# Attention units at experts 23, 32, 40, 45, 53 and 58, with two lists' exponentials beside them, and block 4's list three experts sooner

## Chip, cores and metric

The kernel runs on one core of a Trainium2 chip. The metric is device microseconds of that core; lower is better. Three runs of the kernel before took 1696.72 to 1699.43 us, with a median of 1698.52.

## What is computed

One step of a one-layer decoder, all in float32. There are 512 prompt tokens (four tiles of 128) and 8 sequences of 8 sample tokens (one tile of 64). A token mixer (sliding-window attention with 8 heads beside a gated MLP) and a cross-attention over 256 memory tokens are followed by a retrieval of experts, which takes most of the time:

```python
def block(xt):                                       # 128 tokens
    q = (xt @ w_pq).reshape(128, 8, 2, 128)
    s = einsum('thcd,hckd->thck', q, sub_keys)       # scores of 2 x 128 keys per head
    s1, i1 = top_k(s[:, :, 0], 16); s2, i2 = top_k(s[:, :, 1], 16)
    top, sel = top_k(s1[..., :, None] + s2[..., None, :], 16)
    gate = softmax(top)                              # idx: the 16 chosen of 128*128 experts
    h = einsum('td,thkd->thk', xt, u_tab[idx])
    return einsum('thk,thkd->td', gelu(h) * gate, v_tab[idx])
```

Each token and head has its own 16 rows of the two expert tables. The attention of the prompt tiles 2 to 4, which the change moves, is a softmax over a band of 256 keys with a learned sink per head, and then an RMS norm of its rows.

## The kernel before

**Lists and experts.** The retrieval is cut into 36 lists (the program's `BLOCKS`) of 16 experts. Lists 0 to 3 serve the sample tile, two heads at a time on the two halves of the partitions; then eight lists, one per head, serve each prompt tile. An expert of the program, numbered g = 16 b + k from 0 to 575, is one column of a list: 128 tokens, each with one row of 2048 floats (u and v side by side), so 1 MiB. Every engine runs the same loop over g, and each does its share:

- GpSimd issues the indirect gather (line 684) into one of the slots, after it has waited for the list's indices (`idx_ready`, once for each list) and for the product that used the slot before (`v_used`). `slot_table` (line 407) hands out the slots; from expert 31 to 73 there are eight in turn, so gather g follows the product of expert g - 8.
- VectorE waits for the landing and takes the dot with the token rows (line 1543).
- ScalarE takes Gelu (line 954), multiplies with the gate (958) and writes a 64-wide diagonal (963): `diagonal`, line 949.
- TensorE adds diagonal times v rows to the tile's sum, eight matmuls at line 2118. Its end is `v_used`.

**What is written between them.** The rest of the work stands in the same loops at expert numbers written out by hand. A list n is selected while earlier ones run: `query_at(n)` (line 452) is (n - 2)*16 plus `LATE`, and `query_steps` gives the steps counted from there. TensorE computes the queries at steps 0 to 7 (line 1878), transposes at 9 and scores at 11; ScalarE copies at 9, 11 and 13; VectorE sorts the two key halves at 15 and 16 (`top_keys`, lines 1330 to 1334), takes the best pairs at 18 (`best_pairs`, line 1342, from 1348 to 1351), the experts' indices at 20 (`experts_of`, line 1353; its last instruction, 1371, is `idx_ready`) and finishes the gates at 23 (`finish_gates`, line 1374). ScalarE takes the exponentials of the gates at step 21 (`gates`, line 859), at the head of the expert, ahead of its diagonal. With `LATE` 8 for list 4 its steps start at expert 40: indices at 60, exponentials at 61, finished at 63.

**The six attention units** (`UNIT_AT`, line 430) are tiles 2, 3 and 4, with four heads each. Counted from a unit's expert: TensorE's scores at 0; VectorE's mask and maximum at 4 (four of line 1478, three small ones); ScalarE's exponentials at 5 (line 934), after the diagonal; TensorE's transposes at 6 (line 2080), ScalarE's copies at 8 (940, 941), TensorE's products with the values at 9 (2087), VectorE's scaled output at 12 (1497). A tile's second unit also has the norm of its rows on ScalarE at 13 (lines 945, 946), VectorE's scaling at 16 (`attn_scaled`, line 1319), TensorE's transposes at 18 (1909) and VectorE's `attn_take` at 21 (line 1325). The second unit of the next tile waits for it (`n_T`) ahead of its transposes at 6:

```python
                    if r == 1:
                        pe.wait_ge(n_T, t - 1)
```

**Other work there.** Tile 1's norm ahead of its experts (`ffn`): ScalarE at expert 28 (lines 768, 769), after any unit's work of that expert; VectorE at 30 (lines 1300 and 1305), which waits for it; TensorE's transposes at 31 and 34 (2010) and ScalarE's copies at 33 and 36 (907). On VectorE the steps of a list come before those of a unit of the same expert. ScalarE's functions Gelu, Exp and Sqrt each need their table; a load (ACT_TABLE_LOAD) stands ahead of the first call after another of the three. SP's queue reloads x rows and `w_piece` after unit 5's norm.

Of the kernel before, what the change touches and what calls it, by code (L numbers as in the profile page):

```python
# [117 lines left out]
def hybrid_step(nc, I, O):  # L118
    ctx = ExitStack()
    with ctx:  # L120
# [23 lines left out]
        def bank(n, w=512):  # L144
            return ps[:, n * 512:n * 512 + w]

        def v3(ap, a):
            return ap.rearrange("p (a b) -> p a b", a=a)
# [278 lines left out]
        QUERY_AT = {1: 6, 2: 134, 3: 208, 4: 218}  # L427
        CROSS_AT = {1: 9, 2: 138, 3: 222, 4: 244}
        FFN_AT = {1: 28, 2: 158, 3: 268, 4: 16 * 23 + 2}
        UNIT_AT = (24, 31, 38, 44, 51, 57)  # L430
        OUT_AT = (77, 81, 85, 91, 95, 99, 105, 109, 113, 119, 123, 127)

        LATE = {2: 9, 4: 8, 12: 7}
        QUICK = (2, 12)

        def half_bank(t):
# [15 lines left out]
        def query_at(s):  # L452

            return (s - 2) * TOPK + LATE.get(s, 0)

        def query_steps(g):

            steps = []
            for s in range(BLOCKS):
                d = g - query_at(s)  # L460
                if s in QUICK and 0 <= d < KD // 2:
                    steps += [(s, 2 * d), (s, 2 * d + 1)]
                elif s in QUICK and KD // 2 <= d < 2 * TOPK:
                    steps.append((s, d + KD // 2))
                elif s not in QUICK and 0 <= d < 2 * TOPK:
                    steps.append((s, d))
            return steps

        def units():

            return ((2 + u // 2, u % 2, u, at) for u, at in enumerate(UNIT_AT))

# [217 lines left out]
        def _(act):  # L690
# [27 lines left out]
            def gates_out(t):  # L718

                act.wait_ge(pgu_done, NTH[t])  # L720
                if t == ORDER[0]:
                    act.wait_ge(mkv_done, 2)
                act.wait_ge(x_rstd, NTH[t])
                r = gate_rows(t)
                act.activation(gu_rows(t)[r], bank(gates_bank(t))[r], ACT.Gelu, scale=rs_x[r, t:t + 1]).then_inc(gu_out, 1)
# [31 lines left out]
            def half_norm(t):  # L757

                act.wait_ge(sgu_out, TILES if t == 3 else t + 1)
                spare = gv_rows(4 if t == 3 else t)  # L760
                chain(act.activation(spare, gu_rows(t), ACT.Square, accum_out=ss_g[:, t:t + 1]))
                act.activation(ss_g[:, t:t + 1], ss_g[:, t:t + 1], ACT.Sqrt, bias=eps[:, 0:1], scale=1.0 / 512)\
                   .then_inc(h_std, 1)
# [81 lines left out]
            def queries_out(s):  # L845
                act.wait_ge(pq_q, s + 1)
                act.activation(q_sb, bank(4)[:, 0:256], ACT.Copy).then_inc(pq_qo, 1)

            def queriesT_out(s):
                act.wait_ge(pq_t, s + 1)  # L850
                act.activation(qT_sb, v3(bank(5)[:, 0:256], 2), ACT.Copy).then_inc(pq_to, 1)

            def scores_out(s):
                act.wait_ge(pq_s, s + 1)
                if s > 0:
                    act.wait_ge(best_ready, s)
                act.activation(ss, v3(bank(5)[:, 256:512], 2), ACT.Copy).then_inc(pq_so, 1)  # L857

            def gates(s, m):

                act.wait_ge(best_ready, s + 1)
                act.activation(gate[:, m, :], bestv, ACT.Exp, bias=negtop, accum_out=esum).then_inc(gexp_ready, 1)  # L862
# [34 lines left out]
            def ffn(t, part):  # L897

                if part == 0:
                    act.wait_ge(l_add, 2 * t)  # L900
                    if t >= 2:
                        act.wait_ge(u_used, tile_end(t - 2))
                    row_norm(t, xn(t), f_std, ss_f)
                elif part in (5, 8):
                    h = (part - 5) // 3
                    act.wait_ge(f_tr, 2 * t + h)
                    act.activation(expert_T(t)[:, 4 * h:4 * h + 4, :], v3(bank(6), 4), ACT.Copy).then_inc(f_out, 1)
# [21 lines left out]
            def unit(t, r, u, step):  # L929

                if step == 5:
                    act.wait_ge(a_max, u + 1)
                    for i in range(4):
                        act.activation(U_s[:, i, :], U_s[:, i, :], ACT.Exp, bias=nmx[:, 4 + i:5 + i],
                                       accum_out=rs[:, 4 + i:5 + i])
                    act.activation(es[:, 4:8], es[:, 4:8], ACT.Exp).then_inc(a_exp, 1)
                elif step == 8:
                    act.wait_ge(a_pT, u + 1)
                    act.wait_ge(*((a_pv, u) if u > 0 else (l_pv, 2)))
                    act.activation(U_p[:, 0:4, :], v3(bank(7), 4), ACT.Copy).then_inc(a_pTo, 1)  # L940
                    act.activation(U_p[:, 4:8, :], v3(bank(6), 4), ACT.Copy)\
                       .then_inc(a_pTo, 1)
                elif step == 13 and r == 1:
                    act.wait_ge(a_o, 2 * (t - 1))
                    chain(act.activation(U_p[:, 0:4, :], v3(OU, 4), ACT.Square, accum_out=ss_a[:, t:t + 1]))
                    act.activation(ss_a[:, t:t + 1], ss_a[:, t:t + 1], ACT.Sqrt, bias=eps[:, 0:1], scale=1.0 / 512)\
                       .then_inc(n_std, 1)

            def diagonal(b, k):

                g = b * TOPK + k
                col = slice(k, k + 1)
                act.wait_ge(u_used, g + 1)
                act.activation(hgelu[:, b % 2, col], hdot[:, b % 2, col], ACT.Gelu).then_inc(gelu_ready, 1)  # L954
                if k == 0:
                    act.wait_ge(gate_ready, b + 1)
                act.wait_ge(gelu_ready, g + 1)
                act.activation(coef[:, b % 2, col], gate[:, b % 4, col], ACT.Copy, scale=hgelu[:, b % 2, col])\  # L958
                   .then_inc(coef_ready, 1)
                if g >= DIAGS:  # L960
                    act.wait_ge(v_used, g - DIAGS + 1)
                act.wait_ge(coef_ready, g + 1)
                act.activation(diag[:, g % DIAGS, :], fold[:, 0:HALF], ACT.Copy, scale=coef[:, b % 2, col])\  # L963
                   .then_inc(diag_ready, 1)

            def final(t):

                act.wait_ge(acc_added, t + 1)
                spare = expert_T(1 if t == 3 else 2)
                chain(act.activation(spare, v3(xr(t), KD), ACT.Square, accum_out=stat[:, 64 + t:65 + t]))  # L970
                act.activation(stat[:, 64 + t:65 + t], stat[:, 64 + t:65 + t], ACT.Sqrt, bias=eps[:, 0:1],
                               scale=1.0 / D).then_inc(fin_std, 1)

            act.wait_ge(ld_ffn, 32)
            for b in range(BLOCKS):
                for k in range(TOPK):
                    g = b * TOPK + k
                    for n, step in query_steps(g):
                        if step == 9 and n > 1:
                            queries_out(n)  # L980
                        if step == 11 and n > 1:
                            queriesT_out(n)
                        if step == 13 and n > 1:
                            scores_out(n)
                        if step == 21:
                            gates(n, n % 4)
                    if k == 9 and b in FINAL_SLOT:
                        final(FINAL_SLOT[b])
                    diagonal(b, k)
                    if g == 2:  # L990
                        gates_out(3)
                    if g == 6:
                        gates_out(4)
                    if g == 8:
                        half_norm(3)
                        half_norm(4)
                    if g == 9:
                        qkT_evac(3)
                    if g == 11:
                        qkT_evac(4)  # L1000
                    for t, at in CROSS_AT.items():
                        cross(t, g - at)
                    for t, r, u, at in units():
                        unit(t, r, u, g - at)
                    for t in PREP_AT:
                        if g == PREP_AT[t]:
                            prep(t, 0)
                        if g == QUERY_AT[t] + 2 + (t > 1):
                            prep(t, 3)
                    for t, at in FFN_AT.items():  # L1010
                        ffn(t, g - at)
# [1173 lines left out]
```

## Time and profile before

| | |
|---|---|
| median of three runs | 1698.52 us |
| the profiled execution | 1697.96 us |
| its span, first to last instruction | 1696.2 us |
| granted TensorE clock, mean | 0.861 |
| bytes moved by GpSimd's queue | 604.28 MB, 86.3% of 16 DMA engines' time |
| HBM read | 653.24 MB; 388 GB/s over the span with the writes |
| experts (GpSimd's gathers at line 684) | 566 into R, 10 into x_res |

The experts' loop begins at 172.8 us, with the first gather. The profile gives busy time of the engines, a table of any stretches, and a timeline of each engine in which an instruction's idle time before it and what ended that stand in brackets. A dot (line 1543) is written in the text with its expert's number, which is its place in the order of those instructions.

### The profile page before, as it was taken

The numbers are of one execution on the slowest core, as the hardware profiler recorded it, in microseconds if no ns is written. First come the engines' busy times: TensorE is split into PE (matmuls) and PEld (weight loads), VectorE is DVE, ScalarE is ACT, GpSimd is POOL, SyncE is SP. The second block draws the span as 40 slices with busy tenths as digits, with TensorE's granted clock in tenths as the row PEclk, the third lists the DMA queues.
The fourth block names the chain that finished last, engine by engine and source line by source line (L and its number), as shares of the span: only waits on it lengthen the run. The fifth ranks groups of instructions, "written<-read, shape, count | busy, mean of one in ns | idle before, by whom it ended". The sixth has DMA issues, their size and how long they took to land.

```text
span 1696.2 us, 21662 instructions
## 1 busy us (share of the span) xinstructions
PE 1307.6 (77%) x7069; PEld 474.2 (28%) x7069; DVE 1165.1 (69%) x2798; ACT 806.8 (48%) x2337; POOL 656.4 (39%) x584
## 2 busy tenths in 40 slices
PE   9998987877888777678787776777677677766776
PEld 4454442333344222123232111212112111111110
DVE  2545749797667676777777677677666676777764
ACT  1424456774445454455555454445444445444443
POOL 0000234434534344444444444444444444444441
PEclk9999998989999788988988777877878877788865
DMA  9426799999999999999999999999999999999995
GB/s 359 165 100 251 274 388 420 414 374 421 420 421 421 417 394 414 422 405 412 421 420 421 421 421 421 421 422 420 421 421 422 421 406 421 422 421 420 421 418 220
DMA packets 97441, 657.88 MB, mean 388 GB/s; under 512 B 12512, under 2 KB 15584, under 8 KB 20768
## 3 DMA queue, kind: packets, MB, share of 16 engines
q0 software_dynamic: 83056, 604.28, 86.3%
q1 hardware_dynamic: 14272, 52.21, 8.0%
q8 instruction: 56, 0.92, 0.2%
q14 instruction: 57, 0.47, 0.1%
HBM read 653.24 MB, written 4.19 MB: 388 GB/s over the span
## 4 chain that ended last, share of the span: by engine, by line
DMA 44%; PE 25%; DVE 12%; ACT 11%; issue 7%; POOL 1%; ACTq 0%; DVEq 0%; POOLq 0%
DMA R<-in_peer_uv,R 42%; PE ps L2118 9%; PE ps L1624 5%; DVE R L1543 5%; PE ps L1878 3%; ACT L954 2%; ACT R L963 2%; ACT R L958 1%; PE ps L1595 1%; DVE R L1331 1%; ACT R L954 1%; DVE R L1332 1%; DVE R L1334 1%; ACT L862 1%; POOL R L684 1%
## 5 line engine op out<-in xcount | busy, mean ns | idle before, releaser
L2118 PE MATMUL ps<-R 64*64 64x512 f32 x4528 | 741.5, 736 | 355.8 <-ACT R L963 355.6
L684 POOL DMA_INDIRECT R<-in_peer_uv,R x566 | 643.6, 1137 | 830.7 <-PE ps L2118 754.1
L1543 DVE CUSTOM_DVE_ANT_0 R<-R 128x1024 f32<-128x1024 f32 x566 | 687.8, 1224 | 374.1 <-DMA R<-in_peer_uv,R 370.3
L954 ACT ACTIVATE R<-R 128x1 f32<-128x1 f32 x576 | 115.8, 201 | 602.0 <-DVE R L1543 600.7
L2118 PEld LDWEIGHTS ps<-R 64*64 64x64 f32 x4528 | 136.4, 151 | 710.2 <-ACT R L963 624.2
L963 ACT ACTIVATE R<-R 128x64 f32<-128x64 f32 x576 | 200.4, 348 | 54.9 <-ACT R L958 1.9
L1878 PE MATMUL ps<-A,R 128*128 128x256 f32 (+1 forms) x640 | 221.0, 470 | 0.7 <-ACT R L839 0.7
L958 ACT ACTIVATE R<-R 128x1 f32<-128x1 f32 x576 | 169.7, 295 | 20.9
L1878 PEld LDWEIGHTS ps<-A,R 128*128 128x128 f32 (+1 forms) x640 | 94.8, 198 | 256.1 <-issue 253.1
L1624 PE MATMUL ps<-A,R 128*128 128x512 f32 (+1 forms) x256 | 100.7, 545 | 0.4 <-ACT R L735 0.4
L1595 PE MATMUL ps<-R 128*128 128x256 f32 (+2 forms) x352 | 79.8, 382 | 0.0
L954 ACT ACT_TABLE_LOAD x61 | 78.3, 1283 | 1.5 <-DVE R L1543 0.5
L1595 PEld LDWEIGHTS ps<-R 128*128 128x128 f32 x352 | 60.9, 202 | 23.5 <-issue 15.5
L1624 PEld LDWEIGHTS ps<-A,R 128*128 128x128 f32 x256 | 47.2, 190 | 47.0 <-issue 43.5
L684 POOL DMA_INDIRECT x_res<-in_peer_uv,R x10 | 10.4, 1036 | 119.2 <-DVE R L1383 109.3
L1543 DVE DVE_READ_ACCUMULATOR2_ANT R<- 128x1 f32 x576 | 47.4, 82 | 0.0
L862 ACT ACT_TABLE_LOAD x34 | 43.6, 1283 | 0.6
L1333 DVE MAX8 R<-R 128x8 f32<-128x128 f32 (+1 forms) x106 | 36.1, 340 | 3.7
L1330 DVE MAX8 R<-R 128x8 f32<-128x128 f32 (+1 forms) x106 | 35.7, 337 | 1.5 <-ACT R L857 0.3
L1331 DVE FIND_INDEX8 R<-R 128x8 uint32<-128x128 f32 (+1 forms) x106 | 35.0, 330 | 0.0
L1334 DVE FIND_INDEX8 R<-R 128x8 uint32<-128x128 f32 (+1 forms) x106 | 35.0, 330 | 0.0
L1332 DVE MATCH_REPLACE8 R<-R 128x128 f32<-128x128 f32 (+1 forms) x106 | 34.0, 321 | 0.0
(304 smaller groups left out, 947.5 us busy)
## 6 DMA issues: line engine op xcount, KB each, us to landing
R<-in_peer_uv,R POOLq DMA_INDIRECT x566, 15.6
A<-in_w_pq SPq DMA_DIRECT2D x8, 1024.0 KB, 9.8
A<-in_w_in SPq DMA_DIRECT2D x3, 2048.0 KB, 20.2
R<-in_w_out SPq DMA_DIRECT2D x4, 1024.0 KB, 9.0
x_res<-in_x_prompt SPq DMA_DIRECT2D x6, 512.0 KB, 8.6
R<-in_w_out_rows SPq DMA_DIRECT2D x1, 3072.0 KB, 9.9
R<-in_x_promptT SPq DMA_DIRECT2D x4, 512.0 KB, 7.3
R<-in_w_cq SPq DMA_DIRECT2D x2, 1024.0 KB, 10.7
```

What stands on the lines that cost most here:

```text
L684: pool.indirect_dma_start(slots[slot_of[g]], None, I["peer_uv"][:, :], bass.IndirectOffsetOnAxis(ap=idx[:, b % 4, k:k + 1], axis=0)).then_ ...
L862: act.activation(gate[:, m, :], bestv, ACT.Exp, bias=negtop, accum_out=esum).then_inc(gexp_ready, 1)
L954: act.activation(hgelu[:, b % 2, col], hdot[:, b % 2, col], ACT.Gelu).then_inc(gelu_ready, 1)
L958: act.activation(coef[:, b % 2, col], gate[:, b % 4, col], ACT.Copy, scale=hgelu[:, b % 2, col])\
L963: act.activation(diag[:, g % DIAGS, :], fold[:, 0:HALF], ACT.Copy, scale=coef[:, b % 2, col])\
L1331: chain(dve.max_index(inds[:, 0:8], vals[:, 0:8], values))
L1334: return dve.max_index(inds[:, 8:16], vals[:, 8:16], values)
L1543: dve.tensor_tensor_reduce(u, u, xn(t), 1.0, 0.0, ALU.mult, ALU.add, hdot[:, b % 2, k:k + 1]).then_inc(u_used, 1)
L1595: ins = pe.matmul(out, lhs(k), rhs(k), start=(k == 0), stop=(k == n - 1))
L1624: ins = pe.matmul(out_bank[:, 0:CHUNKS[c][1] - CHUNKS[c][0]], tile_T(t)[:, k, :], w_in[c][:, k, :], start=(k == 0), stop=(k == KD - 1))
L1878: ins = pe.matmul(bank(4)[rows, 0:256], expert_T(t)[:, k, :], w_pq(h)[:, k, :], start=(k == 0), stop=(k == KD - 1))
L2118: ins = pe.matmul(bank(2 * (t % 2) + q)[rows], diag[tokens, g % DIAGS, :], v_rows[slot_of[g]][tokens, c * 512:(c + 1) * 512], start=first, ...
```

## The change

The units start at experts 23, 32, 40, 45, 53 and 58 instead of 24, 31, 38, 44, 51 and 57. List 4's steps start at 37 instead of 40. Exponentials of a list's gates that are due at the expert at which a unit's exponentials stand are taken just ahead of those, behind the diagonal and not ahead of it; with these numbers that holds for list 3 (expert 37, unit 1) and list 4 (expert 58, unit 4).

```diff
-        UNIT_AT = (24, 31, 38, 44, 51, 57)
+        UNIT_AT = (23, 32, 40, 45, 53, 58)
         OUT_AT = (77, 81, 85, 91, 95, 99, 105, 109, 113, 119, 123, 127)
 
-        LATE = {2: 9, 4: 8, 12: 7}
+        LATE = {2: 9, 4: 5, 12: 7}
...
+            def exps_beside(g):
+
+                return any(g - at == 5 for at in UNIT_AT)
+
...
-                        if step == 21:
+                        if step == 21 and not exps_beside(g):
                             gates(n, n % 4)
...
                     for t, r, u, at in units():
+                        for n, step in query_steps(g):
+                            if step == 21 and g - at == 5:
+                                gates(n, n % 4)
                         unit(t, r, u, g - at)
```

## Rows read from the trace of the kernel before

**Rows 1.** The page, busy time of the engines and share of the span.

```profile
PE 1307.6 (77%) x7069; PEld 474.2 (28%) x7069; DVE 1165.1 (69%) x2798; ACT 806.8 (48%) x2337; POOL 656.4 (39%) x584
```

**Rows 2.** Table by stretches: length, busy us (count) by engine, PEclk, DMA share, GB/s.

```profile
360.00:365.00 5.00, 3.87 (x19) 1.16 (x20) 4.83 (x15) 4.60 (x14) 1.96 (x2) 0.66 0.30 102
365.00:370.00 5.00, 4.77 (x44) 2.84 (x42) 4.76 (x19) 4.69 (x12) 3.75 (x5) 1.00 0.96 357
370.00:375.00 5.00, 1.04 (x9) 0.16 (x8) 4.76 (x16) 4.83 (x15) 2.37 (x2) 1.00 1.00 400
...
434.00:574.00 140.00, 118.66 (x668) 57.20 (x664) 93.90 (x221) 58.61 (x181) 56.53 (x50) 0.93 1.01 421
```

**Rows 3.** Line 684, issue to landing; GpSimd's timeline: start, us, instruction [idle <-releaser].

```profile
DMA to landing us min/median/max: 5.5/15.1/20.8
...
312.05 0.94 POOL L684 DMA_INDIRECT R<-in_peer_uv,R  x1 [1.72 <-PE ps L2118]
...
362.73 1.14 POOL L684 DMA_INDIRECT R<-in_peer_uv,R  x1 [9.01 <-DVE R L1371]
...
380.13 0.94 POOL L684 DMA_INDIRECT R<-in_peer_uv,R  x1 [7.09 <-PE ps L2118]
```

**Rows 4.** TensorE's timeline, 300 to 400 us.

```profile
315.49 0.70 PE L1878 MATMUL ps<-A,R 128*128 128x256 f32 x2
...
375.97 1.94 PE L2080 MATMUL ps<-ident,R 128*128 128x128 f32 x8 [4.93 <-DVE R L1325]
```

**Rows 5.** VectorE's timeline, 270 to 384 us.

```profile
273.06 1.22 DVE L1543 CUSTOM_DVE_ANT_0 R<-R 128x1024 f32<-128x1024 f32 x1
...
281.96 0.16 DVE L1300 RECIPROCAL stat<-stat 128x1 f32<-128x1 f32 x1
...
283.35 1.22 DVE L1543 CUSTOM_DVE_ANT_0 R<-R 128x1024 f32<-128x1024 f32 x1
...
296.27 0.42 DVE L1478 CUSTOM_DVE_ANT_0 R<-ps,band 128x256 f32<-128x256 f32 x1
...
302.51 1.21 DVE L1543 CUSTOM_DVE_ANT_0 R<-R 128x1024 f32<-128x1024 f32 x1
...
314.57 0.49 DVE L1497 TENSOR_TENSOR R<-ps,stat 128x128 f32<-128x128 f32 x2 [0.20 <-PE ps L2087]
...
320.54 1.23 DVE L1543 CUSTOM_DVE_ANT_0 R<-R 128x1024 f32<-128x1024 f32 x1 [1.25 <-DMA R<-in_peer_uv,R]
...
342.89 1.23 DVE L1543 CUSTOM_DVE_ANT_0 R<-R 128x1024 f32<-128x1024 f32 x1 [1.24 <-DMA R<-in_peer_uv,R]
...
352.83 1.22 DVE L1543 CUSTOM_DVE_ANT_0 x_res<-x_res,R 128x1024 f32<-128x1024 f32 x1
...
357.06 1.23 DVE L1543 CUSTOM_DVE_ANT_0 R<-R 128x1024 f32<-128x1024 f32 x1
...
359.77 0.17 DVE L1355 TENSOR_SCALAR R<-R 128x16 uint32<-128x16 uint32 x1
...
362.38 0.16 DVE L1319 RECIPROCAL stat<-stat 128x1 f32<-128x1 f32 x1
...
375.14 0.69 DVE L1325 TENSOR_TENSOR R<-ps,gains 128x512 f32<-128x512 f32 x1
```

**Rows 6.** ScalarE's timeline, 264 to 420 us.

```profile
280.27 0.29 ACT L769 ACTIVATE stat<-stat,eps 128x1 f32<-128x1 f32 x1
...
300.54 1.28 ACT L934 ACT_TABLE_LOAD   x1
301.83 0.51 ACT L934 ACTIVATE R<-R,stat 128x256 f32<-128x256 f32 x1
...
306.08 0.20 ACT L954 ACTIVATE R<-R 128x1 f32<-128x1 f32 x1
...
355.60 0.20 ACT L954 ACTIVATE R<-R 128x1 f32<-128x1 f32 x1
...
360.10 0.20 ACT L954 ACTIVATE R<-R 128x1 f32<-128x1 f32 x1
```

## Prediction

> **What bounds the kernel now.** I read the page's busy shares first. No compute engine is above 77% [rows 1], so a wait or a transfer sets the end. The table by stretches says which: from expert 82 on (434 to 574 us) the gathers move 421 GB/s with all 16 DMA engines busy [rows 2]. At 1 MiB each that is 2.49 us per expert, and the vector engine's dots show the same pace. Bytes are fixed, so from expert 20 on the end moves only by the time the DMA engines stand empty. Near the attention units they do so once: 102 GB/s in 360 to 365, 357 and 400 in the next two stretches [rows 2]. (421-102)x5 + (421-357)x5 + (421-400)x5 kB over 421 GB/s is 4.8 us. So the change can win about 4.8 us, 0.28%, while a loss has no such cap. A measurement of this kernel tells about 0.2%, 3.4 us, from no change.
>
> GpSimd's timeline says who made the hole: after gather 63 it waits 9.01 us for L1371, list 4's indices, and issues gather 64 at 362.73 [rows 3]. The same view holds a second cause behind the first. With eight slots in turn, gather g reuses the slot of expert g-8 and waits for its product. Gather 71 goes out at 380.13 after 7.09 us of waiting for TensorE. TensorE was late there because unit 5's transposes waited 4.93 us for L1325 [rows 4], unit 3's `attn_take`, which VectorE reached at 375.14, busy in nearly all of each stretch from 360 on [rows 2, 5].
>
> **The loop as a budget.** VectorE waited on landings for experts 46 and 55 (320.54, 342.89) [rows 5]; that fixes the undisturbed landing of any expert g: 342.89 + 2.49(g-55). Gather 71 is due on VectorE at 382.7; issued at 380.13 after a loss of 4.8 it came at 387.5, a lead of 7.3 us. Bounds: the shortest issue to landing is 5.5 [rows 3]; gather 46 had 8.5 (312.05 to 320.54) and nothing was lost. I take 7.3, from a row in which the stream was just cut. A gather issued later than its due time less 7.3 costs the excess.
>
> **Removed: table loads.** One load is 1.28 us and the next instruction starts 0.01 us behind it (300.54, 301.83 [rows 6]). Gelu, Exp and Sqrt each reload. Unit 0's exponentials (now at expert 28) stand before tile 1's norm: one load fewer. Unit 1's norm and unit 2's exponentials meet at 45: one fewer. Unit 3's norm, list 4's and unit 4's exponentials meet at 58: three instead of six. List 3's exponentials already followed unit 1's with no load between (experts 36 and 37), so that half of the edit buys nothing. In all 5x1.28 = 6.4 us of ScalarE. I keep 6.4, from the rows. The Trainium skill (ScalarE: Activation LUTs, "What ACT_TABLE_LOAD costs") puts 2.66 us on a switch, a drain included, which would make it 13.3 us; the rows show no drain. ScalarE is off the path most of the time; what counts is where its blocks now stand.
>
> **Moved: the first region, experts 28 to 46.** Today the norm's square root is out at 280.56 and VectorE, arriving at 281.96, does not wait [rows 5, 6]. After: unit 0's scores at expert 27 put dot 28 at 276.3 (273.06 + 1.15 + 2.0; the unit step is four L1478, 0.35 apart, and three small ones of 0.2 [rows 5]). ScalarE then does diagonal 28 (to 278.5), load and exponentials (3.6), square (1.2), load and root (1.6): root out at 284.8. VectorE stands from 281.3, and dot 31 starts at 286.4 instead of 283.35: 3.0 late. From there to dot 37 it has no gap (283.35 to 302.51, 19.2 us [rows 5]) and the same steps to do, so dot 37 starts at 305.5. The unit's exponentials, which today run at 300.54 while VectorE is busy [rows 6], now stand behind diagonal 37: 307.8, plus the 5.1 us that the block takes today (300.54 to 306.08 less a 0.5 us copy), so Gelu 38 is at 312.9 and diagonal 38 at 313.8. Product 38 ended at 311.8, just ahead of gather 46 [rows 3]; it will end at 315.0, or 315.9 if TensorE's granted clock has fallen (it stood idle; the stretch 360 to 365 shows 0.66 after such a pause, at the 1.2 GHz level for part of it [rows 2]). Gather 46 is issued 0.3 later, due 320.54 - 7.3 = 313.2. Loss 2.1 to 3.0; I take 2.6. Unit 1's output scaling then waits for TensorE where it waited 0.20 us (314.57 [rows 5]): about 5 us of VectorE pause at expert 44. The landings, late too, and seven light experts absorb it by 52.
>
> **Moved: the second region, experts 52 to 72** (times as if the first cost nothing). List 4's index is ready after dot 57. From dot 52 at 335.4 VectorE has six dots (6.9), two key sorts (3.7), best pairs (dot 58 at 352.83, 1.15 long, to dot 59 at 357.06: 3.1), experts_of (359.77 to 362.38, 2.6 [rows 5]) and unit steps (3.9): index at 353.1, dot 58 at 355.6. Due for gather 64 is 365.3 - 7.3 = 358.0, so the 9.01 us wait is gone and with it this hole. But all of list 4's selection, unit 3's outputs and unit 4's scores now precede dot 58, which was at 352.83. Behind it ScalarE has one block: the diagonal (1.0), the norm (355.60 to 360.10 today, less that and a load: 2.2), and gates and exponentials as a 5.1 us block like the one above: 8.3 us from Gelu 58 to Gelu 59 [rows 6]. The gates' sums are out 4.9 us after Gelu 58 (356.9: 1.0 + 2.2 + 1.3 + 0.4), at 361.8; `finish_gates` at dot 60 wants them at 359.1. VectorE waits 2.7 us for gates that today are taken before diagonal 61, with no norm and no unit ahead of them. Dot 61 at 362.1; five dots (5.8), two sorts for list 5 (3.7), unit steps (3.5): dot 66 at 375.1. `attn_take` has moved from 65 to 66, and there stands behind best pairs of list 5: 1.15 + 3.1 + 0.6, done at 380.0 instead of 375.8. Unit 5's transposes, the held product and the next gather follow as they do today, 375.97 to 380.13, 4.2 us [rows 3, 4]: gather 72 is issued at 384.2, due 385.2 - 7.3 = 377.9. Loss 6.3; waits of VectorE for TensorE on the way, the kind that shows as 0.20 us today and grows to 5 in the first region, may add 1.5. I take 7.0.
>
> **Queues.** SP's reload of `w_piece` waits for unit 5's norm, now at expert 71, and feeds a product at 77: its bytes are the same, six experts cover it, and without them it costs TensorE one expert, 2.5 us. List 4's query products on TensorE (37 to 44 instead of 40 to 47) and its three copies on ScalarE keep their number; they lie in waits for diagonals. Without that cover the products cost 0.70 us an expert (315.49 [rows 4]). GpSimd only gains list 4's index earlier.
>
> **Sum.** 2.6 + 7.0 - 4.8 = +4.8 us. The profiled execution took 1697.96 (span 1696.2), 0.6 below the median of the runs; on the median's scale 1703.2.
>
> **Rivals.**
> 1. The stall only changes its name. The first region's delay is absorbed by gathers already queued (lead nearer 5.5), and gather 72 takes over from 64: 7.0 - 4.8 = +2.2, or zero if the pauses are smaller, 1698 to 1701. For it: today's gather 71 was nearly as late as 64, two causes of one hole. Against: gather 46 has only 1.1 us to spare.
> 2. Faster. List 4's work falls into pauses of VectorE (1.24 us before dot 55 [rows 5], more before 54), the saved loads bring products 59 to 64 forward, and no new wait comes: the hole closes by up to 4.8 us, 1693.7. It decides at one point: gather 72 issued by 378. Against it: a grouped block waits for the latest of its inputs and holds up every diagonal behind it. The Trainium skill's rule to group calls by table set (ScalarE: Activation LUTs, "Table sets: the hidden batching unit") is this rival: by it, fewer switches win.
> 3. Both pauses are worse (slow clock at product 38 and 59, exponentials of unit 4 delaying unit 5's scores): 4 + 8.5 - 4.8 = +7.7, 1706.
>
> **Chances.** My forecast with rival 3, 0.57 (0.45 and 0.12); rival 1, 0.30; rival 2, 0.13. Beyond 0.2%: slower 0.57, faster 0.13, within 0.30. The range runs from rival 1's lower end (1698) to rival 3's (1706), each with 2 to 2.5 us for the bounds of the lead and the clock: 1695.5 to 1708. Within my own case: 1701.5 to 1705.
>
> **What would show it.** Right: five fewer table loads on ScalarE; the 9.01 us wait on L1371 gone; L1300 at expert 30 behind a pause of 3 to 4 us for ScalarE; gather 46 at 315 to 316 and a dip of GB/s near 315 to 320; VectorE waiting for L862 at `finish_gates` of list 4; L2080 waiting for L1325 before product 64 and a dip after 370. Wrong: 420 GB/s through both stretches, or dot 37 still at 302.5. Then the end would be 4 to 5 us earlier, not later.

## The result and the profile after

The change made the kernel slower: 1708.65 us, median of five runs (1704.59 to 1715.74), against 1698.52 (1696.72 to 1701.47, five runs beside them). The ratio is 1.0066, with a 95% interval of 1.0044 to 1.0089. Run a second time, beside the experiments, it was 1710.0 against 1700.48: 1.0051, 1.0037 to 1.0065. So the change costs 9.5 to 10.1 us by the medians (8.7 to 11.2 by the ratios) where I forecast 4.8. The sign was right, the size was half, and 1708.65 lies 0.65 above my range.

The profiled execution of the changed kernel took 1715.74 (span 1714.0), the highest of its five times and 7.1 above their median. Its own difference to the one of before, 17.8 us, is therefore larger than the change's cost. The change's second profiled execution took 1717.29, again the longest of its group, and shows the same waits as the first within 0.2 us. So the traces of the change show it at its slow end, while the profiled executions of the other kernels below lie within 3.3 us of their medians. I use the traces for where and why, and the medians for how much. Lines of VectorE and TensorE stand seven lower in the code than before (L1543 is L1550, L2118 is L2125); ScalarE's up to 963 have not moved. The edits of the experiments move them again by up to three lines.

The page, busy time of the engines, to be read beside [rows 1]:

```profile
PE 1317.4 (77%) x7069; PEld 476.6 (28%) x7069; DVE 1164.8 (68%) x2798; ACT 800.8 (47%) x2332; POOL 647.3 (38%) x584
```

ScalarE is down by 6.0 us and five instructions: the five table loads forecast at 6.4 us. The work went down and the time went up, so the loss is waiting. The table by stretches shows it. For the kernel before, experts 37 to 80 or so (columns as in [rows 2]):

```profile
300.00:345.00 45.00, 37.63 (x262) 17.52 (x254) 32.91 (x85) 35.62 (x103) 21.98 (x19) 0.96 1.01 416
345.00:414.00 69.00, 54.22 (x346) 24.07 (x340) 56.52 (x161) 46.73 (x128) 28.58 (x25) 0.93 0.96 391
```

and for the changed kernel the same two stretches, then the first in detail:

```profile
300.00:345.00 45.00, 35.05 (x194) 13.14 (x190) 31.91 (x90) 26.30 (x79) 19.09 (x16) 0.78 0.92 359
345.00:414.00 69.00, 57.22 (x350) 26.28 (x346) 53.36 (x156) 46.77 (x132) 27.08 (x24) 0.87 0.90 343
...
306.00:312.00 6.00, 2.11 (x9) 0.50 (x10) 5.40 (x20) 2.98 (x9) 0.40 (x1) 0.68 1.02 429
312.00:318.00 6.00, 5.05 (x19) 2.32 (x19) 5.44 (x12) 5.60 (x19) 1.78 (x1) 0.50 1.00 406
318.00:324.00 6.00, 6.00 (x28) 2.06 (x28) 0.76 (x2) 3.54 (x14) 2.26 (x2) 0.68 0.73 255
324.00:330.00 6.00, 6.00 (x46) 3.46 (x46) 3.38 (x14) 0.00 (x0) 2.43 (x3) 1.00 0.96 340
...
342.00:350.00 8.00, 8.00 (x49) 3.94 (x49) 3.67 (x12) 6.26 (x19) 3.67 (x4) 0.77 0.79 268
...
356.00:362.00 6.00, 6.00 (x33) 2.20 (x36) 5.79 (x17) 2.70 (x9) 1.87 (x2) 0.72 0.78 291
...
380.00:386.00 6.00, 6.00 (x38) 2.60 (x31) 4.94 (x20) 3.35 (x12) 2.82 (x3) 0.73 0.64 229
```

Against the 421 GB/s of the undisturbed pace, the DMA time lost is (421-416)/421 x 45 + (421-391)/421 x 69 = 0.5 + 4.9 = 5.4 us before, and 6.6 + 12.8 = 19.4 after: 14.0 us more. One hole (102 GB/s, [rows 2]) has become four dips: 255, 268, 291 and 229 GB/s. Another 2.5 us of the profiled difference lie ahead of all that the change touches: the dot at 273.06 [rows 5] starts at 275.56.

VectorE's timeline and then TensorE's behind diagonal 37 of the changed kernel; after 317 us of VectorE, only its main pauses are shown:

```profile
287.08 0.16 DVE L1307 RECIPROCAL stat<-stat 128x1 f32<-128x1 f32 x1 [3.35 <-ACT stat L769]
288.48 1.22 DVE L1550 CUSTOM_DVE_ANT_0 R<-R 128x1024 f32<-128x1024 f32 x1
...
307.60 1.23 DVE L1550 CUSTOM_DVE_ANT_0 R<-R 128x1024 f32<-128x1024 f32 x1
...
326.51 0.49 DVE L1504 TENSOR_TENSOR R<-ps,stat 128x128 f32<-128x128 f32 x2 [7.75 <-PE ps L2094]
...
346.82 0.29 DVE L1337 MAX8 R<-R 128x8 f32<-128x128 f32 x1 [2.82 <-ACT R L857]
...
374.72 0.16 DVE L1383 RECIPROCAL stat<-stat 128x1 f32<-128x1 f32 x1 [3.29 <-ACT R L862]
```

```profile
309.89 1.99 PE L2125 MATMUL ps<-R 64*64 64x512 f32 x8 [4.74 <-ACT R L963]
311.81 1.22 PE L1885 MATMUL ps<-A,R 128*128 128x256 f32 x2
313.67 1.97 PE L2087 MATMUL ps<-ident,R 128*128 128x128 f32 x8 [0.64 <-ACT stat L936]
315.95 1.98 PE L2125 MATMUL ps<-R 64*64 64x512 f32 x8 [0.31 <-ACT R L963]
317.86 1.22 PE L1885 MATMUL ps<-A,R 128*128 128x256 f32 x2
319.01 1.99 PE L2125 MATMUL ps<-R 64*64 64x512 f32 x8
320.93 1.10 PE L1885 MATMUL ps<-A,R 128*128 128x256 f32 x2
...
323.03 1.09 PE L2125 MATMUL ps<-R 64*64 64x512 f32 x8
324.05 0.70 PE L1885 MATMUL ps<-A,R 128*128 128x256 f32 x2
324.58 1.89 PE L2094 MATMUL ps<-R 128*128 128x64 f32 x16
...
379.35 1.99 PE L2125 MATMUL ps<-R 64*64 64x512 f32 x8 [0.58 <-ACT R L963]
...
394.32 1.94 PE L2087 MATMUL ps<-ident,R 128*128 128x128 f32 x8 [4.85 <-DVE R L1332]
```

GpSimd's timeline, gathers 46, 67 and 72; the wait of 9.01 us for list 4's indices [rows 3] is gone:

```profile
318.24 1.32 POOL L684 DMA_INDIRECT R<-in_peer_uv,R  x1 [4.28 <-PE ps L2125]
...
381.64 1.31 POOL L684 DMA_INDIRECT R<-in_peer_uv,R  x1 [6.92 <-PE ps L2125]
...
398.47 1.83 POOL L684 DMA_INDIRECT R<-in_peer_uv,R  x1 [7.13 <-PE ps L2125]
```

Every wait that I had named is there: 3.35 us for the norm's root, the long pause at expert 44, `finish_gates` behind line 862, unit 5's transposes behind `attn_take`. One is there that I had not named: 6.92 us ahead of gather 67, which follows product 59 (379.35 above, at 1.99 us), and with it the deepest dip, 229 GB/s. The experiments ask which of them cost the time.

### The profile page after: what moved, and what is told of

It reads as the page before. It is cut to its first block, busy times and chain, and to the rows that moved or that the text cites. A ratio compares the mean times of both kernels' runs of the same rounds, so it can differ in the third digit from the quotient of the medians.

```text
span 1714.0 us, 21658 instructions
## 1 busy us (share of the span) xinstructions
PE 1317.4 (77%) x7069; PEld 476.6 (28%) x7069; DVE 1164.8 (68%) x2798; ACT 800.8 (47%) x2332; POOL 647.3 (38%) x584
## 4 chain that ended last, share of the span: by engine, by line
DMA 43%; PE 25%; DVE 12%; ACT 11%; issue 7%; POOL 1%; SPq 1%; ACTq 0%; DVEq 0%; POOLq 0%
DMA R<-in_peer_uv,R 41%; PE ps L2125 10%; DVE R L1550 5%; PE ps L1885 4%; PE ps L1631 4%; ACT L954 2%; ACT R L963 2%; DMA R<-in_mem_prompt 1%; ACT R L958 1%; PE ps L1602 1%; ACT L862 1%; DVE R L1338 1%; DVE R L1339 1%; DVE R L1341 1%; ACT R L954 1%
## 5 line engine op out<-in xcount | busy, mean ns | idle before, releaser
L2125 PE MATMUL ps<-R 64*64 64x512 f32 x4528 | 747.2, 741 | 360.0 <-ACT R L963 359.7
L684 POOL DMA_INDIRECT R<-in_peer_uv,R x566 | 634.0, 1120 | 857.7 <-PE ps L2125 790.1
L1550 DVE CUSTOM_DVE_ANT_0 R<-R 128x1024 f32<-128x1024 f32 x566 | 687.6, 1225 | 369.1 <-DMA R<-in_peer_uv,R 364.6
L2125 PEld LDWEIGHTS ps<-R 64*64 64x64 f32 x4528 | 136.2, 151 | 715.5 <-ACT R L963 626.8
L1885 PE MATMUL ps<-A,R 128*128 128x256 f32 (+1 forms) x640 | 225.3, 479 | 0.7 <-ACT R L839 0.7
L1550 DVE DVE_READ_ACCUMULATOR2_ANT R<- 128x1 f32 x576 | 47.3, 82 | 0.0
```

Of the source, the lines that this page charges most:

```text
L684: pool.indirect_dma_start(slots[slot_of[g]], None, I["peer_uv"][:, :], bass.IndirectOffsetOnAxis(ap=idx[:, b % 4, k:k + 1], axis=0)).then_ ...
L1550: dve.tensor_tensor_reduce(u, u, xn(t), 1.0, 0.0, ALU.mult, ALU.add, hdot[:, b % 2, k:k + 1]).then_inc(u_used, 1)
L1885: ins = pe.matmul(bank(4)[rows, 0:256], expert_T(t)[:, k, :], w_pq(h)[:, k, :], start=(k == 0), stop=(k == KD - 1))
L2125: ins = pe.matmul(bank(2 * (t % 2) + q)[rows], diag[tokens, g % DIAGS, :], v_rows[slot_of[g]][tokens, c * 512:(c + 1) * 512], start=first, ...
```

## The experiments

All times of one group were taken beside runs of the kernel before. GB/s is the row 300 to 414 us of the table by stretches of the profiled execution (before: 401); since the experts' loop starts up to 4.3 us apart from one execution to the next (172.69 to 176.99), I read only differences of 10 or more in it.

| kernel | median us | before | ratio, 95% | GB/s |
|---|---|---|---|---|
| list 4 sooner alone | 1703.57 | 1701.08 | 1.0014, 1.0003 to 1.0024 | 380 |
| units and exponentials alone | 1706.2 | 1701.08 | 1.0032, 1.0022 to 1.0043 | 380 |
| change, unit 0 back at 24 | 1711.07 | 1701.08 | 1.0059, 1.0044 to 1.0074 | 355 |
| change, norm ahead of the exponentials | 1710.9 | 1701.08 | 1.0055, 1.0042 to 1.0068 | 370 |
| the change again | 1710.0 | 1700.48 | 1.0051, 1.0037 to 1.0065 | 348 |
| change, gates back at the head | 1710.83 | 1700.48 | 1.0062, 1.0048 to 1.0075 | 355 |
| change, `attn_take` first at 66 | 1705.61 | 1700.48 | 1.0041, 1.0027 to 1.0055 | 379 |
| change, products at 41 to 44 | 1705.68 | 1700.48 | 1.0029, 1.0020 to 1.0039 | 367 |
| change, both repairs | 1701.84 | 1700.93 | 1.0008, 0.9997 to 1.0019 | 385 |
| list sooner, products at 41 to 44 | 1701.64 | 1700.93 | 1.0006, 0.9994 to 1.0018 | 392 |
| the same, gates finished at 62 | 1701.45 | 1700.93 | 1.0006, 0.9995 to 1.0018 | 389 |
| change, products all at 37 to 40 | 1712.63 | 1700.93 | 1.0075, 1.0061 to 1.0089 | 361 |

### One half at a time

The kernel before with list 4's steps from 37:

```diff
-        LATE = {2: 9, 4: 8, 12: 7}
+        LATE = {2: 9, 4: 5, 12: 7}
```

> The kernel before with list 4's steps at 37 alone; the units stay. Theory (pauses): the harm of the change is in where the units' exponentials stand, so this part alone does no harm. GpSimd's 9.01 us wait for L1371 is gone, the wait ahead of gather 71 (7.09 us) stays because attn_take stays at expert 65; finish_gates of list 4 waits under 1 us. 1694 to 1699 us, 0 to 4 under the kernel before. Rival (the earlier list itself loads VectorE too much ahead of dot 58): 1702 or more.

The changed kernel with list 4 back at 40 (the same two lines, the other way round):

> The changed kernel with list 4's steps back at 40 (its gates stand alone at 61; list 3's stay beside unit 1's). Theory (pauses): the first region's chain is whole: VectorE waits 3 to 3.5 us for the norm's root at expert 30 and 5 us or more for unit 1's products at expert 44; 1703 to 1710 us. Rival (list 4 and its gates beside unit 4 are most of the harm): within 3 us of the kernel before.

The list alone was to gain and lost 2.5 us (1.0003 to 1.0024), and `finish_gates`, which was to wait under 1 us, waits 3.04. Its 9.01 us wait is gone, so removing the wait that stood ahead of the hole bought nothing. The units alone cost 5.1 us, as expected. The two differences sum to 7.6, the whole costs 9.5 to 10.1: the intervals are too wide to say whether they come to more together.

In the kernel with the list alone, three pairs of the list's query products (experts 37 to 39) stand ahead of unit 1's value products at 40; in the changed kernel it is four (37 to 40). The first of the three in its TensorE timeline:

```profile
310.01 1.22 PE L1878 MATMUL ps<-A,R 128*128 128x256 f32 x2
```

The pair costs 0.70 us at full clock [rows 4] and 1.22 here (the other two 0.70). VectorE waits 2.40 us for those value products at expert 43; before the change it was 0.20 [rows 5].

### The norm's wait at expert 30

Unit 0 back at 24, and, separately, tile 1's norm ahead of unit 0's exponentials on ScalarE:

```diff
-        UNIT_AT = (23, 32, 40, 45, 53, 58)
+        UNIT_AT = (24, 32, 40, 45, 53, 58)
```

> The changed kernel with unit 0 back at 24, so that its exponentials follow the norm of tile 1. Theory (pauses): the wait for the norm's root at expert 30 falls from 3.35 us to under 0.5, dot 37 starts about 3 us sooner against the landings, the wait for unit 1's products at 44 falls under 4 us; 1701 to 1705 us, some 4 to 7 under the changed kernel. Rival (the second region, experts 52 to 72, is nearly all of the loss): 1707 or more.

```diff
+                    if g == FFN_AT[1]:
+                        ffn(1, 0)
                     for t, r, u, at in units():
...
                     for t, at in FFN_AT.items():
-                        ffn(t, g - at)
+                        if g != FFN_AT[1] or t != 1:
+                            ffn(t, g - at)
```

> The changed kernel with tile 1's norm ahead of unit 0's exponentials on ScalarE at expert 28; every place is kept. Theory (pauses): as with unit 0 at 24, since only the order on ScalarE counts: the wait at expert 30 goes under 1 us, 1701 to 1705 us. Rival (unit 0's earlier place delays VectorE or TensorE by itself): stays at 1707 or more though the wait is gone.

The pause of 3.35 us was gone in the first and shrank to 0.53 in the second (VectorE's timeline of that kernel):

```profile
281.97 0.16 DVE L1310 RECIPROCAL stat<-stat 128x1 f32<-128x1 f32 x1 [0.53 <-ACT stat L769]
...
321.55 0.49 DVE L1507 TENSOR_TENSOR R<-ps,stat 128x128 f32<-128x128 f32 x2 [4.88 <-PE ps L2097]
```

The time did not move: 1711.07 and 1710.9, with the change's own 1710.0 in the next group, where I expected 1701 to 1705. The pause that is easiest to see in the timeline adds nothing that was measured. The pause at expert 44 falls without it, but most of it stays (5.81 us in the first kernel, 4.88 here, 7.75 in the change), so the dots being 3 us late are at most a part of it.

### Three repairs of the change

The change again, for a value beside them:

> The changed kernel itself, on the same chip and beside the same runs of the kernel before as the three that follow. All theories: 1.004 to 1.009 of the kernel before; VectorE waits 2.5 to 3.5 us for list 4's gates at expert 60 and about 3.3 us for the norm's root at 30.

Exponentials of all lists ahead of the diagonal again:

```diff
-                return any(g - at == 5 for at in UNIT_AT)
+                return False
...
-                        for n, step in query_steps(g):
-                            if step == 21 and g - at == 5:
-                                gates(n, n % 4)
                         unit(t, r, u, g - at)
```

> The changed kernel with the exponentials of all lists at the head of their expert again; all places kept. ScalarE has two table loads more at expert 58 (2.6 us), but list 4's sums are out before diagonal 58. Theory (late inputs of a grouped block): the 3.3 us wait at expert 60 is gone, and since the loads now stand ahead of diagonal 58 part of it comes back there; 0 to 3 us under the changed kernel. Rival (table loads are what counts): 2 to 4 us above it.

Unit 3's `attn_take` ahead of best pairs of list 5 in expert 66:

```diff
-                elif step == 21 and r == 1:
+                elif step == 21 and r == 1 and u != 3:
                     attn_take(t)
...
+                    if g == UNIT_AT[3] + 21:
+                        attn_take(3)
                     for n, step in query_steps(g):
```

> The changed kernel with unit 3's attn_take ahead of list 5's best pairs on VectorE at expert 66. Theory (take behind best pairs holds TensorE before product 64): it is done 3.1 us sooner, gather 72 goes out about 3 us sooner, and the loss of DMA time at experts 71 to 74 falls by 2 to 3 us; 1.5 to 3 us under the changed kernel. Rival (the loss there is decided earlier, by the lateness of dot 58): under 1 us.

List 4's query products (steps 0 to 7, experts 37 to 44) two steps an expert at 41 to 44:

```diff
-                        if n > 1 and step < KD:
+                        if n > 1 and step < KD and n != 4:
                             w = len(heads_of(n))
                             q_mm(n, w * step, w * step + w)
+                        if n == 4 and 4 <= step < KD:
+                            w = 2 * len(heads_of(n))
+                            q_mm(n, w * (step - 4), w * (step - 4) + w)
```

> The changed kernel with list 4's query products on TensorE at experts 41 to 44, two steps in each, instead of one step in each of 37 to 44; everything else of list 4 keeps its place. Theory (these products stand ahead of unit 1's value products at 41, where TensorE is slow and late): VectorE's wait for L2094 at expert 44 falls by 3 us or more, the loss of DMA time at experts 37 to 50 falls by 2 us, 2 to 4 us under the changed kernel. Rival (cover is there, as the prediction had it): no difference over 1 us.

**Gates at the head.** 1710.83, the change's own time within the intervals; neither the theory (0 to 3 us less) nor the rival (2 to 4 more) is shown. This kernel has four table loads more than the change (59 at line 954 and 6 at line 934, against 57 and 4; I had expected two), 4 x 1.28 = 5.1 us of ScalarE, and is not measurably slower. The wait of 3.29 us at `finish_gates` is gone from it, but VectorE waits 2.93 us for the norm at the next expert and 2.80 for unit 4's exponentials right behind it. Loads and order changed together here, so the run doesn't price a load by itself. The Trainium skill's rule to group calls by table set (ScalarE: Activation LUTs, "Table sets: the hidden batching unit") is not borne out here as a gain in time: the grouped kernel has the fewer loads and is as long.

Its TensorE timeline behind product 37 bears on the reading of the first region:

```profile
311.19 1.99 PE L2122 MATMUL ps<-R 64*64 64x512 f32 x8 [4.77 <-ACT R L963]
...
316.96 1.09 PE L2122 MATMUL ps<-R 64*64 64x512 f32 x8 [1.19 <-ACT R L963]
...
322.87 1.89 PE L2091 MATMUL ps<-R 128*128 128x64 f32 x16
```

The query products stand at 37 to 44 as in the change, yet product 38 ran at full speed, the value products started 11.7 us after product 37 (322.87 less 311.19) and VectorE's pause at expert 44 was 4.43 us. The kernel is no faster for it.

**`attn_take` first.** 4.4 us less by the medians, where 1.5 to 3 were expected; but the intervals of the ratios (1.0027 to 1.0055, and 1.0037 to 1.0065 for the change) overlap widely, so this run alone doesn't show it. TensorE's timeline shows the wait that it was aimed at, 4.85 us in the change, at 1.47:

```profile
387.84 1.06 PE L2089 MATMUL ps<-ident,R 128*128 128x128 f32 x8 [1.47 <-DVE R L1332]
```

and GpSimd waits 2.33 us ahead of gather 72 instead of 7.13 (the longest behind it is 3.83). The wait ahead of gather 67 stays, at 7.55.

**Products at 41 to 44.** 4.3 us less, with nothing taken away: the same 16 matmuls, moved. Its interval (1.0020 to 1.0039) and the change's just meet. TensorE's timeline behind diagonal 37:

```profile
311.02 1.99 PE L2125 MATMUL ps<-R 64*64 64x512 f32 x8 [4.76 <-ACT R L963]
314.79 1.97 PE L2087 MATMUL ps<-ident,R 128*128 128x128 f32 x8 [1.79 <-ACT stat L936]
317.07 3.34 PE L2125 MATMUL ps<-R 64*64 64x512 f32 x16 [0.32 <-ACT R L963]
...
321.41 1.09 PE L2125 MATMUL ps<-R 64*64 64x512 f32 x8
322.43 2.00 PE L2094 MATMUL ps<-R 128*128 128x64 f32 x16
```

The value products start 11.4 us after product 37 (322.43 less 311.02) instead of 14.7 (324.58 less 309.89). VectorE's pause at 44 falls from 7.75 to 4.61, and the dip at 342 to 350, 268 GB/s in the change, is gone:

```profile
318.00:324.00 6.00, 6.00 (x46) 2.95 (x39) 1.85 (x4) 4.56 (x16) 2.92 (x3) 0.84 0.76 269
...
342.00:350.00 8.00, 6.19 (x45) 3.77 (x43) 5.36 (x22) 7.57 (x22) 3.47 (x3) 1.00 1.02 408
```

The first dip (255 in the change, 269 here) stays, and so does the one at 356 to 362 (291, and 300 here); what goes is the dip between them. That the earlier value products are what saves the time is argued, not shown: the kernel with the gates at the head has them as early and saves nothing.

### Both repairs, the list alone repaired, and the cost made worse

The changed kernel with the last two diffs together:

> The changed kernel with both repairs of the last group at once: list 4's query products two steps an expert at 41 to 44, and unit 3's attn_take at expert 66 ahead of list 5's best pairs. Each alone gave 4.3 to 4.4 us under the changed kernel (1705.7 and 1705.6 against 1710.0). If the two losses lie in two places that add up (products: experts 37 to 50; attn_take: experts 66 to 78), the time is 1700.5 to 1702.5, the kernel before's within 2 us. If both repairs only shift the same late chain, or if a delay of the first region is carried into the second and counted in both, it stays at 1704 to 1706.

1701.84, as the first theory had it. Against the change's 1710.0 that is 8.2 us (8.6 if the 0.45 between the two groups' times of before is taken off), where 4.4 and 4.3 make 8.7. Each repair also shows beside the other: with `attn_take` first, moving the products takes the ratio from 1.0041 to 1.0008, and with the products moved, `attn_take` first takes it from 1.0029 to 1.0008, and neither pair of intervals overlaps. By the medians the two losses add up. The DMA time lost, worked out as above from the profiled executions, puts them mainly in two places:

| kernel | 300 to 345 us | 345 to 414 us |
|---|---|---|
| before | 0.5 | 4.9 |
| the change, two executions | 6.6, 5.8 | 12.8, 13.9 |
| `attn_take` first | 5.2 | 6.2 |
| products at 41 to 44 | 3.2 | 11.3 |
| both | 2.9 | 6.7 |
| gates at the head | 3.6 | 14.1 |

With both repaired, the changed kernel cannot be told from the one before (0.9997 to 1.0019). Its wait ahead of gather 67 is still 6.91 us.

The kernel before with the list sooner and its products at 41 to 44:

> The kernel before with list 4 three experts sooner (units where they were), but list 4's query products at 41 to 44, two steps an expert, instead of 37 to 44. The list alone was 2.4 us slower than the kernel before. Theory: that was its products at 37 to 39 ahead of unit 1's value products at 40, at the lower granted clock; without them the closed hole (9.01 us wait, 4.8 us of DMA time) should show: 1697 to 1699.5, ratio 0.998 to 0.999 of the kernel before, and VectorE's wait for L2087 at expert 43 (2.40 us) under 1. Rival: the list's own steps on VectorE, 15 to 23 at experts 52 to 60, are what costs (finish_gates waits 3.04 us at 60): 1702 to 1704, and the wait at 43 makes no difference.

1701.64, between the two: the wait at expert 43 fell from 2.40 to 1.12 us and 300 to 345 us is near its full rate (411 GB/s against 392 with the list alone), so the products' place may have cost something here as well; the intervals of the two kernels (1.0003 to 1.0024, and 0.9994 to 1.0018) overlap. But no gain came. The table by stretches and GpSimd's timeline say why:

```profile
360.00:366.00 6.00, 4.92 (x36) 2.16 (x34) 4.83 (x11) 5.82 (x16) 2.52 (x3) 1.00 0.95 375
...
372.00:378.00 6.00, 6.00 (x44) 3.77 (x40) 4.08 (x13) 3.64 (x12) 2.48 (x2) 0.71 0.72 255
...
384.00:390.00 6.00, 4.99 (x26) 2.03 (x26) 5.73 (x18) 2.66 (x8) 1.03 (x2) 0.72 0.84 318
```

```profile
372.52 1.54 POOL L684 DMA_INDIRECT x_res<-in_peer_uv,R  x1 [6.17 <-PE ps L2118]
...
388.54 0.93 POOL L684 DMA_INDIRECT R<-in_peer_uv,R  x1 [6.46 <-PE ps L2118]
```

The hole at 360 (102 GB/s, [rows 2]) is gone; 255 at 372 and 318 at 384 stand in its place, behind waits of 6.17 and 6.46 us for TensorE. The stall changed its name.

The same, with list 4's gates finished two experts later:

```diff
-                        if step == 23:
+                        if step == (25 if n == 4 else 23):
                             finish_gates(n, n % 4)
```

> As the kernel before it here (list 4 sooner, products at 41 to 44, units where they were), and finish_gates of list 4 at expert 62 instead of 60; its gates are first needed by diagonal 64. This takes away VectorE's wait of 3.04 us for the exponentials at expert 60. If that wait delays product 64 and gather 72 as in my reading of the second region, 1 to 3 us less than the kernel with the products moved only: 1694.5 to 1698. If dots are ahead enough there, no difference (within 1 us).

1701.45: no difference, where 1 to 3 us were expected. The wait of 2.96 us at expert 60 is gone from VectorE's timeline; in its place stand 1.29 us for the unit's norm at the same expert and 2.22 instead of 1.12 for the scores at 63. VectorE only reached sooner what ScalarE had not done yet. The wait at `finish_gates` shows that ScalarE is late, it does not make it late.

And the change with its products packed at 37 to 40, two steps an expert:

> The changed kernel with the suspected cost made worse: list 4's query products all at 37 to 40, two steps an expert, where TensorE comes out of its pause behind diagonal 37 and unit 1's transposes and value products stand. If these products are what cost 4.3 us in the changed kernel, packing them here costs 2 to 4 us more: 1712 to 1714, VectorE's wait at expert 44 9 to 10 us instead of 7.6. If what counts is only how much TensorE has to do in the region as a whole, the time stays at 1709 to 1711 and the wait at 44 stays as it is.

1712.63, in the expected range and 2.6 above the change; but the intervals (1.0061 to 1.0089, and 1.0037 to 1.0065) overlap, so a cost isn't shown. The row that was to go with it did not come: the wait at 44 is 5.40, not 9 to 10. TensorE's timeline, and then the table by stretches for its clock:

```profile
311.01 1.99 PE L2125 MATMUL ps<-R 64*64 64x512 f32 x8 [4.75 <-ACT R L963]
312.93 2.07 PE L1885 MATMUL ps<-A,R 128*128 128x256 f32 x4
314.79 1.18 PE L2087 MATMUL ps<-ident,R 128*128 128x128 f32 x8
317.06 1.09 PE L2125 MATMUL ps<-R 64*64 64x512 f32 x8 [1.09 <-ACT R L963]
```

```profile
312.00:318.00 6.00, 4.91 (x28) 2.34 (x20) 4.95 (x13) 5.68 (x21) 1.77 (x1) 0.75 1.01 415
```

With twice as many matmuls behind product 37 the granted clock was back at full speed by product 38 (1.09 us, where the change has 1.98 and again 1.99 for product 39). The number of matmuls did not decide that: the kernel with the gates at the head has two behind product 37, as the change has, and was back by product 38 too. So this run is at most weak support for the theory in its time, and speaks against its mechanism. Where its 2.6 us went, if they are real, is open.

## Why the prediction was wrong in size

**Right.** The five loads, with no drain behind them: in the change `L769` starts 0.01 us after its load ends. The 9.01 us wait gone. The first region up to gather 46: taking off the 2.5 us by which this execution starts late, dot 31 is at 286.0 (forecast 286.4), dot 37 at 305.1 (305.5), gather 46 at 315.7 (315.3 to 316.2), and VectorE waited 3.35 us for the root (forecast 3.5). `finish_gates` waits 3.29 us (2.7). `attn_take` stands behind best pairs and TensorE waits for it; putting it ahead gave 4.4 us back. That this is near the 4.2 us that I had worked out for its delay (380.0 for 375.8) is in part luck: of these only the 3.1 us of best pairs can be won by the order.

**The step that failed** is the cover in "Queues": list 4's query products "lie in waits for diagonals", and so cost nothing. The reading was wrong already for the kernel before. Where its query products begin, TensorE has no waits:

```profile
318.00:324.00 6.00, 6.00 (x44) 2.63 (x36) 3.60 (x7) 5.80 (x14) 3.55 (x3) 1.00 1.01 419
```

They cost nothing there because the gathers went out early enough all the same: VectorE waits for landings at that time (1.25 us for expert 46 [rows 5]). At 37 to 40 that slack is gone: they stand where TensorE comes out of the pause that the same change makes, in its two profiled executions at the clock's lower level (0.50 in 312 to 318; in the kernel before 0.72 in 306 to 312 and then 1.00). Moving them off these experts was worth 4.3 us. I had written the price of the lost cover, 0.70 us an expert, and not asked whether my own first region took the cover away. Nor is it the price: in the changed kernel three of the four pairs took 1.22, 1.22 and 1.10. That the place costs 4.3 us is shown; by which chain it does is not. The slow clock and the late value products are not shown to be it: the profiled execution of the kernel with the gates at the head has neither, and that kernel is as long. It loses less DMA time ahead of 345 us (3.6 us against 6.6 and 5.8) and as much behind.

**The step that fell with it** is "The landings, late too, and seven light experts absorb it by 52". VectorE's pause at 44 was 7.75 us, not 5, and the delay was still there at 52: a wait of 2.82 us for list 4's scores and a dip of 268 GB/s in 342 to 350, where I had no loss at all. The kernel with the products moved waits 0.24 us there and has 408 GB/s. So the first region was sized at 2.6 us from gather 46 alone, the first late gather, as if those behind it came on time.

**Sum by the runs.** By the medians: products' place 4.3, `attn_take`'s place 4.4, and 0.9 (not distinguishable from nothing) for all the rest: 9.6 us, against 9.5 to 10.1 measured. In my sum 2.6 + 7.0 - 4.8, the missing 4.7 to 5.3 us are about the products' term. The rest of that sum is not confirmed by this: beside `attn_take` it has 2.6 for the first region, 2.6 for the second and -4.8 for the hole, which come to about nothing, and no run shows one of the three by itself. That they cancel is as good as luck.

**The gain of 4.8 us** for the closed hole is not seen as such: the list alone, even with its products out of the way, is at 1.0006 (0.9994 to 1.0018). One place where it may have gone is the wait of 6.9 us ahead of gather 67, which my second region passed over and which the kernel with both repairs still has; no run removes it. Rival 1's mechanism, a stall that changes its name, fits that half. It failed for the whole because it let the first region's delay be absorbed. Rival 2 (faster) is out. Rival 3 named two things that the change's traces show, a slow clock at products 38 and 59 (1.98 and 1.99 us), and was the nearest in time (1706), still 2.65 short.

**My explanation of the wait at expert 30** as the head of the first region's loss is out: without the wait the time was the same.

**Open.** The lead of 7.3 us was not tested by itself, and the row that it comes from is weaker than I wrote: that gather 71 landed at 387.5 is worked out, not seen, for dot 71 started at 390.64 without waiting. Where the crowded kernel lost its time is not known. That the changed kernel scatters from 1704.59 to 1717.29 us may come from when the clock returns (both profiled executions of it, 1715.74 and 1717.29, had TensorE at 0.50 and then 0.60 to 0.68 in 312 to 324), but none of its shorter executions was profiled. The kernel with `attn_take` first, the same up to expert 66, had 0.50 and then 0.87 in an execution of 1703.34.

No version here beats the kernel before; the three that equal it are within 0.12% of it.

## What to carry to other kernels

When an edit moves several things at once, check each "hidden" term against the schedule that the other edits make, not against the old one: a cover that lasted in the old trace can be what the change itself uses up. Size a stall by every transfer behind it until the stream has caught up, not by the first late one. And before closing the widest wait in a timeline, look for what is late next: taking a 9 us wait away gained nothing here, and some 4 us lay in the order of two steps within one expert.

## What the hardware showed that I had not expected

- After an idle stretch of 4.74 us TensorE ran at the 1.2 GHz level, as the rows of eight matmuls at 1.98 to 1.99 us against 1.09 show. When full speed came back was not the same each time, and the number of matmuls queued there does not order it. With two matmuls of the list behind product 37, the products 38 and 39 took 1.98 and 1.99 us in the change (1.99 twice in its second execution), 1.99 and 1.25 with `attn_take` first, and 1.09 twice with the gates at the head. With four they took 1.09 twice. With none the two took 3.34 together, 3.58 with both repairs and 2.60 with list 4 back at 40. This is one execution of each, two of the change. So a small matmul behind such a pause cost 0.6 or 0.35 us (1.22 or 0.70 a pair), and the trace of one execution can't tell which it will be in the next.
- Four table loads more or less (5.1 us of ScalarE), together with another order of the exponentials, made no difference in time, and 3.35 us of VectorE waiting made none, in a kernel in which removing most of 4.85 us of TensorE waiting gave some 4 back. Which engine stands still says little; what counts is which gather it holds up.
